# Ten small products go from VectorE to GpSimd, three weight low parts come back, and six selection steps stand earlier

## The chip, the cores and the metric

One core of one Trainium2 chip runs one program. The metric is the time of the program on the device in microseconds (us), median of several runs.

## What is computed

Two layers of a decoder trunk over 512 positions of width 1024. Each layer is `x + token_mix(rms_norm(x))`, then `x + mlp(rms_norm(x))` with a squared ReLU and 4096 hidden columns. The token mixing projects the normed input once and cuts the result into 14 parts, for three groups of heads:

```python
proj = h @ w_in
(g_q, g_k, g_v, g_gate, g_lr, d_q, d_k, d_v, i_q, i_k, i_w, m_cq, m_ckv, m_kr) = split_columns(proj)
# gated linear attention: log_a = log_sigmoid(g_lr @ up + bias) / 16; b = cumsum(log_a) in chunks of 64
q_dec = qc * exp(b);  k_inv = kc * exp(-b);  k_end = kc * exp(b_end - b)
# sparse attention: score[t,s] = sum_h iw[t,h] * relu(iq[t,h] . ik[s]); each query keeps its top 128 causal keys
_, idx = lax.top_k(score, top_k)
# latent attention: q_m = rms_norm(rms_norm(m_cq) @ w_uq), k_m likewise from m_ckv and m_kr, rotary on 32 columns of each
return jnp.concatenate([o_gla, o_dsa, o_mla], axis=-1) @ w_out
```

## The kernel before

All tensors live in SBUF with features on partitions and the 512 positions along the row. The weights of a layer come in 96 units of 128 x 1024 words in a fixed order: 24 for the input projection (`UNITS`, `N_IN`), 8 for the output projection, 64 for the MLP. SyncE loads each unit into one of two `raw` buffers. A unit is split in two: ScalarE writes its rounded high part `wh` (L952, semaphore `hi_ready`), and another engine the low part `wl = raw - wh` (`lo_ready`). TensorE then makes 3 products for each of 8 blocks of a unit (L517 to L519: low by high, high by high, high by low), 24 for a unit, into one of 8 PSUM banks. Split and use are two units apart (`AHEAD`). Low parts are made by VectorE (`low_part`, L1275) for units 0 to 7 and for those of the output projection and the MLP, and by GpSimd (L464) for the units that are used two after those in `POOL_LOW = range(6, N_IN)`, that is from 8 on.

Each engine has one queue, written out by hand and run in order. In slot `u` (0 to 23) of the input projection:

- ScalarE waits until TensorE is through with unit `u`, splits unit `u + 2`, and does its `tasks(u)`: ReLU planes for the indexer (`relevant`), squares for the norms (`square`), factors `rsqrt(mean + eps)` (`factor`, `key_factor`), the exponentials of the decays (slot 8, into `e1` and `e2`, `exp_ready`), and a scaled copy of each latent query into `tf` (`query_square`, `q_copied`).
- VectorE takes the unit out of its bank (`evacuations`), makes some selection steps (`select_steps`), and does its own `tasks(u)`: the weighted sums of the indexer's planes (`weighted`, L1401), the scan for the decays (L1478, L1480), the normed queries and keys of the sparse heads (`dsa_queries` L1362, `dsa_keys` L1367) and of the latent heads (`mla_turn`, `mla_queries`, `mla_keys`).
- TensorE runs unit `u`, and between units small fp32 products: sums of squares for the norms (`stat`, L553; the one for the key factor L608, L609), `mla_q(h)` (L587, L589), `mla_k(pr)` (L600) and `mla_v(i)` (L618). Its order is `unit(9)`, `dqst0`, `mla_q(0)`, `unit(10)`, `mqst0`, `dqst1`, `mla_q(1)`, ..., `unit(15)`, `mkst1`, `mla_v(0)`, `unit(16)`, `mla_v(1)`, `unit(17)`.

A bank is used again when its readers have freed it. `mla_v(1)` writes the bank that held `mk1`, and that is freed by the second product of `mla_keys(1)`:

```python
vec.scalar_tensor_tensor(kT[0:NOPE, 2 * pr + 1], mk[NOPE:P, :], gain(G_MKN, NOPE, P), f[NOPE:P],
                         ALU.mult, ALU.mult).then_inc(*B.on_read(f"mk{pr}"))        # L1389
```

`mla_v(0)` and `mk0` are tied in the same way. A selection step finds the 8 largest scores of each of 128 queries (MAX8, L1350) and replaces them by a mark (a MATCH_VALUE_LOAD and a MATCH_REPLACE8, L1354). 16 steps for each of the query blocks 3, 2 and 1 (rows of 512, 384 and 256 scores) make 48; in before they go round in the order 3, 2, 1, and `per_slot` spreads them over slots 9 to 22. Steps of three different blocks are issued together, since they don't wait for one another. After slot 23 come the attention heads, the output projection and the MLP, which the change doesn't touch.

Of the kernel before, what the change touches and what calls it, by code (L numbers as in the profile page):

```python
# [17 lines left out]
ALU = mybir.AluOpType  # L18
# [39 lines left out]
POOL_LOW = range(6, N_IN)  # L58
# [36 lines left out]


# [110 lines left out]
def build_trunk(nc, x_in, stream, params, consts, out):  # L207
    with ExitStack() as ctx:
# [144 lines left out]
        q_copied = S("q_copied", H)  # L353
        krb_ready = S("krb_ready")
# [76 lines left out]
        def _(pool):  # L431
# [18 lines left out]
            for l in range(DEPTH):  # L450
# [9 lines left out]
                pool.memset(gqp[:], 0.0).then_inc(zeroed.sem, 1)  # L460
                pool.wait_ge(*lo_ready.at(l, POOL_LOW[0] + AHEAD - 1))
                for u in POOL_LOW:
                    pool.wait_ge(*hi_ready.at(l, u + AHEAD))
                    pool.tensor_tensor(wl[:, u % 2], raw[:, u % 2], wh[:, u % 2], ALU.subtract)\  # L464
                        .then_inc(lo_ready.sem, 1)
                    if u == 19:
                        pool.wait_ge(*B.filled(l, "mv1"))
                        alone(pool)
                    if u in (19, 21):
                        pool.memset(ke[:, (u - 19) // 2], 0.0).then_inc(zeroed.sem, 1)  # L470
# [790 lines left out]
        def _(vec):  # L1261
# [50 lines left out]
            for l in range(DEPTH):  # L1312
# [27 lines left out]
                def select_steps(first, n):  # L1340


                    for i0 in range(first, first + n, 3):
                        queries = [3 - i % 3 for i in range(i0, min(i0 + 3, first + n))]
                        found = {}
                        for qb in queries:
                            if qb in taken:
                                vec.wait_ge(*taken[qb])
                            alone(vec)
                            found[qb] = mark(vec.max(m8[:, qb - 1], scores_of(qb)))  # L1350
                        for qb in queries:
                            vec.wait_ge(*found[qb])
                            alone(vec)
                            taken[qb] = mark(vec.match_replace(scores_of(qb), m8[:, qb - 1], scores_of(qb), TAKEN))  # L1354
# [15 lines left out]
                def mla_turn(h):  # L1370
                    vec.wait_ge(*q_copied.at(l, h))
                    vec.tensor_tensor(tf[64:QK, h % 2], tf[64:QK, h % 2], cos, ALU.mult)
                    vec.scalar_tensor_tensor(qT[64:QK, h], B[f"mq{h}"][QK:P, :], gain(G_MQ, QK, P), sin,
                                             ALU.mult, ALU.mult).then_inc(*B.on_read(f"mq{h}"))

                def mla_queries(h):

                    vec.wait_ge(*B.freed(l, f"mq{h}"))
                    link(vec.tensor_tensor(tf[64:QK, h % 2], tf[64:QK, h % 2], qT[64:QK, h], ALU.add))
                    f = use_factor(f"mqst{h}")  # L1380
                    after(vec.tensor_tensor(qT[0:QK, h], tf[0:QK, h % 2], f[0:QK], ALU.mult),
                          nrs_used.sem, nrs_used.at(l, norm_index(f"mqst{h}"))[1])
# [22 lines left out]
                def evacuations(u):  # L1405
# [42 lines left out]
                    if u in (12, 13):  # L1448
                        pr = u - 12
                        vec.wait_ge(*exp_ready.at(l, pr))  # L1450
                        vec.wait_ge(*zeroed.at(l, 0))

                        link(vec.scalar_tensor_tensor(kinv[:, pr], rb[:], GLA_DK ** -0.5, e1[:, pr],
                                                      ALU.mult, ALU.mult))
                        vec.wait_ge(*B.filled(l, f"gq{pr}"))
                        vec.tensor_tensor(gqp[0:64, 2 * pr], B[f"gq{pr}"][0:64, :], kinv[0:64, pr], ALU.mult)
                        vec.tensor_tensor(gqp[64:P, 2 * pr + 1], B[f"gq{pr}"][64:P, :], kinv[64:P, pr], ALU.mult)\
                            .then_inc(*B.on_read(f"gq{pr}"))
                    if u in (14, 15):
                        pr = u - 14  # L1460
                        link(vec.tensor_tensor(e2[:, pr], e2[:, pr], rb[:], ALU.mult))
# [6 lines left out]
                def tasks(u):  # L1468
# [5 lines left out]
                    if u == 7:  # L1474
                        weighted(3)
                        for pr in range(2):
# [6 lines left out]
                    if u == 8:  # L1483
                        f = use_factor("cqst")
# [31 lines left out]
                    if u in (14, 15):  # L1516
                        pr = u - 14
                        vec.wait_ge(*B.freed(l, f"gk{pr}"))
                        dec = e1[:, pr].rearrange("p (c t) -> p c t", t=CHUNK)[:, :, CHUNK - 1:CHUNK]
                        vec.tensor_tensor(tf[:, pr].rearrange("p (c t) -> p c t", t=CHUNK),  # L1520
                                          kinv[:, pr].rearrange("p (c t) -> p c t", t=CHUNK),
                                          dec.to_broadcast([P, NCHUNK, CHUNK]), ALU.mult)\
                            .then_inc(kend_ready.sem, 1)
                        mla_keys(pr)

                steps = 3 * (TOPK // 8)
                per_slot = {9: 3, 10: 3, 11: 3, 12: 2, 13: 2, 14: 2, 15: 2, 16: 4, 17: 4, 18: 4,
                            19: 5, 20: 5, 21: 5, 22: 4}
                done = 0
                for u in range(N_IN):  # L1530
                    if u not in POOL_LOW and (l, u) != (0, 0):
                        low_part(u % 2, hi_ready.at(l, u + AHEAD))
                    evacuations(u)
                    select_steps(done, per_slot.get(u, 0))
# [322 lines left out]
```

## Time and profile before

| | us |
|---|---|
| median of 3 runs | 1255.13 (1254.95 to 1256.62) |
| profiled execution, own time | 1253.49 |
| its span, first to last instruction | 1251.7 |
| TensorE busy | 1236.5 |
| VectorE busy | 777.6 |
| ScalarE busy | 528.5 |
| GpSimd busy | 216.7 |

Engines are named in the profile as PE (TensorE), PEld (its weight loads), DVE (VectorE), ACT (ScalarE), POOL (GpSimd) and SP (SyncE). The granted TensorE clock was 0.999 of full speed over the span. Times in rows are microseconds from the start of the span. The shown end of a matmul is modelled and lies over the start of the next; the distance of two starts is the better measure: 0.23 us within a unit.

### The profile page before, as it was taken

Reading aid. Unit: us, or ns where it says so; the run is one execution under the profiler, and the core shown is the slowest. Engines: PE = TensorE matmul, PEld = TensorE weight load, DVE = VectorE, ACT = ScalarE, POOL = GpSimd, SP = SyncE. Lnnn points to the kernel's source line nnn. Section 1 sums busy time; section 2 is a strip of 40 time slices with the busy share of each in tenths; the row PEclk is TensorE's granted clock in tenths of the full one; section 3 lists DMA queues with packets and bytes.
Section 4 is the critical chain, followed back from the end, with each engine's and each line's share of the span. In section 5 each row is a group of like instructions: output and inputs, shape, how many; then the busy total and the mean of one; then the engine's idle time right before and its main releaser. Section 6 shows DMA issues by size and latency. Waiting matters only on the chain.

```text
span 1251.7 us, 17687 instructions
## 1 busy us (share of the span) xinstructions
PE 1236.5 (99%) x5956; PEld 973.0 (78%) x5956; DVE 777.6 (62%) x1234; ACT 528.5 (42%) x858; POOL 216.7 (17%) x140
## 2 busy tenths in 40 slices
PE   8999999999999999999999999999999999999998
PEld 7766776688888888888886667767888888888887
DVE  6699988644644554544757999785446445445444
ACT  5674438643323224224437643585442242232331
POOL 1132330020120110210522234200201102102002
PEclk9999999999999999999999999999999999999999
DMA  6212220023232223322322222201232232233223
GB/s 242 89 51 68 68 85 2 17 102 116 99 101 91 95 98 101 101 84 101 101 89 81 68 68 68 69 2 46 89 101 90 96 101 101 84 101 101 95 98 109
DMA packets 30720, 108.36 MB, mean 87 GB/s; under 512 B 3536, under 2 KB 3536, under 8 KB 30672
## 3 DMA queue, kind: packets, MB, share of 16 engines
q1 hardware_dynamic: 29520, 103.82, 24.9%
q0 software_dynamic: 432, 2.86, 0.6%
q10 hardware_dynamic: 720, 1.07, 0.3%
q8 instruction: 27, 0.44, 0.2%
q14 instruction: 21, 0.17, 0.0%
HBM read 105.64 MB, written 2.10 MB: 86 GB/s over the span
## 4 chain that ended last, share of the span: by engine, by line
PE 82%; DVE 11%; issue 4%; ACT 3%; DMA 1%; ACTq 0%; DVEq 0%
PE bank L898 19%; PE bank L897 19%; PE bank L899 19%; PE bank L517 4%; PE bank L518 4%; PE bank L519 4%; PE bank L540 2%; PE bank L538 2%; PE bank L539 2%; PE bank L779 1%; PE bank L791 1%; DVE sel L1401 1%; PE bank L806 1%; DVE sel L1354 1%; DVE m L1350 1%
## 5 line engine op out<-in xcount | busy, mean ns | idle before, releaser
L952 ACT ACTIVATE wh<-raw 128x1024 fp32r<-128x1024 f32 x191 | 201.7, 1056 | 377.9 <-PE bank L899 246.5
L1275 DVE TENSOR_TENSOR wl<-raw,wh 128x1024 fp32r<-128x1024 f32 x155 | 240.5, 1552 | 75.6 <-ACT wh L952 75.5
L897 PE MATMUL bank<-hh,wl 128*128 128x512 f32 x512 | 200.0, 391 | 0.0
L897 PE MATMUL bank<-xmh,wl 128*128 128x512 f32 x512 | 199.3, 389 | 0.0
L899 PE MATMUL bank<-hl,wh 128*128 128x512 f32 x512 | 199.2, 389 | 0.0
L899 PE MATMUL bank<-xml,wh 128*128 128x512 f32 x512 | 199.2, 389 | 0.0
L898 PE MATMUL bank<-xmh,wh 128*128 128x512 f32 x512 | 199.2, 389 | 0.0
L898 PE MATMUL bank<-hh,wh 128*128 128x512 f32 x512 | 199.2, 389 | 0.0
L482 POOL TENSOR_TENSOR x<-x,rsb 128x512 f32<-128x512 f32 x62 | 82.0, 1322 | 587.4 <-DVE rsb L1696 587.4
L1685 DVE TENSOR_TENSOR sqb<-tf 128x512 f32<-128x512 f32 x64 | 44.3, 692 | 181.6 <-ACT hh L1238 181.6
L517 PE MATMUL bank<-xgh,wl 128*128 128x512 f32 x368 | 151.0, 410 | 2.7 <-DVE xgl L1288 2.5
L519 PE MATMUL bank<-xgl,wh 128*128 128x512 f32 x368 | 143.5, 390 | 0.0
L518 PE MATMUL bank<-xgh,wh 128*128 128x512 f32 x368 | 143.5, 390 | 0.0
L464 POOL TENSOR_TENSOR wl<-raw,wh 128x1024 fp32r<-128x1024 f32 x36 | 87.6, 2432 | 232.3 <-ACT wh L952 232.3
L1236 ACT ACTIVATE tf<-bank 128x512 f32<-128x512 f32 x64 | 38.3, 598 | 204.5 <-PE bank L899 204.5
L1696 DVE TENSOR_TENSOR rsb<-bank,rb 128x512 f32<-128x512 f32 x64 | 44.3, 692 | 128.0 <-PE bank L899 125.8
L897 PEld LDWEIGHTS bank<-hh,wl 128*128 128x128 f32 x512 | 96.1, 188 | 20.5 <-issue 0.5
L897 PEld LDWEIGHTS bank<-xmh,wl 128*128 128x128 f32 x512 | 96.1, 188 | 20.5 <-DVE xml L1288 0.4
L898 PEld LDWEIGHTS bank<-hh,wh 128*128 128x128 f32 x512 | 96.1, 188 | 20.2 <-issue 0.5
L899 PEld LDWEIGHTS bank<-hl,wh 128*128 128x128 f32 x512 | 96.1, 188 | 20.0
L899 PEld LDWEIGHTS bank<-xml,wh 128*128 128x128 f32 x512 | 96.1, 188 | 19.9
L898 PEld LDWEIGHTS bank<-xmh,wh 128*128 128x128 f32 x512 | 96.1, 188 | 19.8
(218 smaller groups left out, 1669.2 us busy)
## 6 DMA issues: line engine op xcount, KB each, us to landing
raw<-in_stream SPq DMA_DIRECT2D x191, 512.0 KB, 3.3
out_y<-x SPq DMA_DIRECT2D x8, 256.0 KB, 3.5
x<-in_x ACTq DMA_DIRECT2D x4, 256.0 KB, 7.0
x<-in_x SPq DMA_DIRECT2D x4, 256.0 KB, 7.1
con<-in_consts POOLq DMA_DIRECT2D x1, 976.5 KB, 5.2
par<-in_params POOLq DMA_DIRECT2D x1, 916.0 KB, 5.5
par<-in_params POOLq DMA_DIRECT2D x1, 896.0 KB, 6.9
raw<-in_stream SPq DMA_DIRECT2D x2, 256.0 KB, 4.1
```

The lines of the kernel that those rows point to most:

```text
L464: pool.tensor_tensor(wl[:, u % 2], raw[:, u % 2], wh[:, u % 2], ALU.subtract)\
L482: pool.tensor_tensor(x[:, d], x[:, d], rsb[:, d % 2], ALU.add).then_inc(x_ready.sem, 1)
L517: pe.matmul(bank[:], wk_l, act_h[:, k], start=(n == 0), stop=False)
L518: pe.matmul(bank[:], wk_h, act_h[:, k], start=False, stop=False)
L519: m = pe.matmul(bank[:], wk_h, act_l[:, k], start=False, stop=last)
L897: pe.matmul(B.t[s][:], wl[:, s, n_block(k)], src_h[:, k], start=(k == 0), stop=False)
L898: pe.matmul(B.t[s][:], wh[:, s, n_block(k)], src_h[:, k], start=False, stop=False)
L899: m = pe.matmul(B.t[s][:], wh[:, s, n_block(k)], src_l[:, k], start=False, stop=(k == KB - 1))
L952: act.activation(wh[:, s], raw[:, s], ACT.Copy).then_inc(hi_ready.sem, 1)
L1275: vec.tensor_tensor(wl[:, s], raw[:, s], wh[:, s], ALU.subtract).then_inc(lo_ready.sem, 1)
L1685: vec.tensor_tensor(sqb[:, s], tf[:, s], tf[:, s], ALU.mult).then_inc(hid_ready.sem, 1)
L1696: vec.tensor_tensor(rsb[:, s], B.t[s][:], rb[:], ALU.mult).then_inc(dn_freed[s].sem, 1)
```

## The change

`POOL_LOW` begins at 9, not 6: in slots 6, 7 and 8 VectorE makes the low parts of units 8, 9 and 10, after its evacuations. GpSimd takes ten products of each layer: the decays `e1` and `e2` times `rb` (two each, `scale_decay`), the cosine part of the four latent queries' rotation (`turn_query`, on 32 partitions), and `kend` (two, `key_end`). They stand in its queue behind its low parts of slots 9 to 15. The factor `GLA_DK ** -0.5` goes into VectorE's products that write `gqp`. Of the selection, two steps of query block 3 are made in slots 7 and 8, one in each; slots 12 to 15 have three steps in place of two, and slots 19 to 22 have 4, 4, 3, 2 in place of 5, 5, 5, 4.

```diff
-POOL_LOW = range(6, N_IN)
+POOL_LOW = range(9, N_IN)
+SELECT = [3, 3] + [3, 2, 1] * (TOPK // 8 - 2) + [2, 1] * 2
...
+        q_turned = S("q_turned", H)
+        scaled = S("scaled", 4)
...
+                def scale_decay(buf, pr):
+                    pool.wait_ge(*exp_ready.at(l, 1))
+                    src, dst = (e1, kinv) if buf == 0 else (e2, e2)
+                    pool.tensor_tensor(dst[:, pr], src[:, pr], rb[:], ALU.mult).then_inc(scaled.sem, 1)
+
+                def turn_query(h, ahead):
+                    pool.wait_ge(*ahead)
+                    pool.wait_ge(*q_copied.at(l, h))
+                    pool.tensor_tensor(tf[64:QK, h % 2], tf[64:QK, h % 2], cos, ALU.mult).then_inc(q_turned.sem, 1)
+                    pool.wait_ge(*q_turned.at(l, h))
+
+                def key_end(pr):
+                    pool.wait_ge(*B.freed(l, f"gk{pr}"))
+                    dec = e1[:, pr].rearrange("p (c t) -> p c t", t=CHUNK)[:, :, CHUNK - 1:CHUNK]
+                    pool.tensor_tensor(tf[:, pr].rearrange("p (c t) -> p c t", t=CHUNK),
+                                       kinv[:, pr].rearrange("p (c t) -> p c t", t=CHUNK),
+                                       dec.to_broadcast([P, NCHUNK, CHUNK]), ALU.mult).then_inc(kend_ready.sem, 1)
+
...
+                    if u == 9:
+                        pool.wait_ge(const_loaded, 16)
+                        scale_decay(0, 0)
+                        scale_decay(0, 1)
+                        turn_query(0, scaled.at(l, 1))
+                    if u in (10, 11):
+                        scale_decay(1, u - 10)
+                        turn_query(u - 9, scaled.at(l, u - 8))
+                    if u == 12:
+                        turn_query(3, lo_ready.at(l, u + AHEAD))
+                    if u in (14, 15):
+                        key_end(u - 14)
...
                 def mla_turn(h):
                     vec.wait_ge(*q_copied.at(l, h))
-                    vec.tensor_tensor(tf[64:QK, h % 2], tf[64:QK, h % 2], cos, ALU.mult)
...
                 def mla_queries(h):
 
                     vec.wait_ge(*B.freed(l, f"mq{h}"))
+                    vec.wait_ge(*q_turned.at(l, h))
...
                     if u in (12, 13):
                         pr = u - 12
-                        vec.wait_ge(*exp_ready.at(l, pr))
+                        vec.wait_ge(*scaled.at(l, pr))
...
-                        link(vec.scalar_tensor_tensor(kinv[:, pr], rb[:], GLA_DK ** -0.5, e1[:, pr],
-                                                      ALU.mult, ALU.mult))
...
-                        vec.tensor_tensor(gqp[0:64, 2 * pr], B[f"gq{pr}"][0:64, :], kinv[0:64, pr], ALU.mult)
...
+                        vec.scalar_tensor_tensor(gqp[0:64, 2 * pr], B[f"gq{pr}"][0:64, :], GLA_DK ** -0.5,
+                                                 kinv[0:64, pr], ALU.mult, ALU.mult)
...
-                        link(vec.tensor_tensor(e2[:, pr], e2[:, pr], rb[:], ALU.mult))
+                        vec.wait_ge(*scaled.at(l, 2 + pr))
...
                     if u == 7:
                         weighted(3)
+                        select_steps(0, 1)
...
                     if u == 8:
+                        select_steps(1, 1)
...
-                per_slot = {9: 3, 10: 3, 11: 3, 12: 2, 13: 2, 14: 2, 15: 2, 16: 4, 17: 4, 18: 4,
-                            19: 5, 20: 5, 21: 5, 22: 4}
-                done = 0
+                per_slot = {9: 3, 10: 3, 11: 3, 12: 3, 13: 3, 14: 3, 15: 3, 16: 4, 17: 4, 18: 4,
+                            19: 4, 20: 4, 21: 3, 22: 2}
+                done = 2
                 for u in range(N_IN):
-                    if u not in POOL_LOW and (l, u) != (0, 0):
+                    if u < 6 and (l, u) != (0, 0):
                         low_part(u % 2, hi_ready.at(l, u + AHEAD))
                     evacuations(u)
+                    if 6 <= u < POOL_LOW[0]:
+                        low_part(u % 2, hi_ready.at(l, u + AHEAD))
                     select_steps(done, per_slot.get(u, 0))
```

`key_end`'s product stood in VectorE's `tasks(14)` and `tasks(15)` (L1520), `turn_query`'s at L1372, `scale_decay`'s at L1453 and L1461.

## Rows read from the trace of the kernel before

**Rows 1.** The page, part 1: busy us, share of the span, instructions.

```profile
...
PE 1236.5 (99%) x5956; PEld 973.0 (78%) x5956; DVE 777.6 (62%) x1234; ACT 528.5 (42%) x858; POOL 216.7 (17%) x140
...
```

**Rows 2.** By stretch: us, busy PE, PEld, DVE, ACT, POOL (instructions), clock, DMA share, GB/s.

```profile
...
62.00:135.00 73.00, 70.81 (x268) 47.95 (x266) 70.30 (x111) 41.18 (x67) 20.90 (x9) 1.00 0.18 58
...
135.00:175.00 40.00, 40.00 (x180) 33.03 (x180) 35.78 (x99) 15.95 (x20) 17.53 (x9) 1.00 0.26 83
...
```

**Rows 3.** TensorE's waits over the whole span: total, times, longest.

```profile
...
PE bank L618 <- DVE kT L1389: 4.4, 2, 2.2
...
```

**Rows 4.** Timeline of TensorE: start, us, operation, idle before and releaser.

```profile
...
132.41 0.39 PE L519 MATMUL bank<-xgl,wh 128*128 128x512 f32 x1
134.99 1.13 PE L618 MATMUL bank<-par,ckvn 128*128 128x256 f32 x4 [2.19 <-DVE kT L1389]
...
```

**Rows 5.** The chain that ended last, 124 to 137 us.

```profile
...
126.19 2.42 DVE kT L1391
...
134.18 0.77 DVE kT L1389
...
```

**Rows 6.** Timeline of GpSimd, 40 to 150 us.

```profile
...
67.28 2.51 POOL L464 TENSOR_TENSOR wl<-raw,wh 128x1024 fp32r<-128x1024 f32 x1 [8.47 <-ACT wh L952]
74.62 2.38 POOL L464 TENSOR_TENSOR wl<-raw,wh 128x1024 fp32r<-128x1024 f32 x1 [4.83 <-ACT wh L952]
82.53 2.36 POOL L464 TENSOR_TENSOR wl<-raw,wh 128x1024 fp32r<-128x1024 f32 x1 [5.53 <-ACT wh L952]
91.46 2.36 POOL L464 TENSOR_TENSOR wl<-raw,wh 128x1024 fp32r<-128x1024 f32 x1 [6.57 <-ACT wh L952]
...
```

**Rows 7.** Timeline of VectorE, 40 to 180 us.

```profile
...
62.70 0.69 DVE L1478 SCALAR_TENSOR_TENSOR e<-tf,e 128x512 f32<-128x512 f32 x1 [1.51 <-ACT e L1088]
...
67.56 3.04 DVE L1401 SCALAR_TENSOR_TENSOR sel<-rel,iws,sel 128x256 f32<-128x256 f32 x2
...
73.75 3.53 DVE L1401 SCALAR_TENSOR_TENSOR sel<-rel,iws,sel 128x256 f32<-128x256 f32 x3
...
77.83 0.69 DVE L1330 TENSOR_TENSOR dqr<-bank,rb 128x512 f32<-128x512 f32 x1
78.44 1.47 DVE L1350 MAX8 m<-sel 128x8 f32<-128x512 f32 x3
...
81.52 0.68 DVE L1372 TENSOR_TENSOR tf<-tf,con 32x512 f32<-32x512 f32 x1
82.22 0.76 DVE L1373 SCALAR_TENSOR_TENSOR qT<-bank,par,con 32x512 f32<-32x512 f32 x1
83.01 2.43 DVE L1362 SCALAR_TENSOR_TENSOR dqn<-dqr,par,rsb 128x512 f32<-128x512 f32 x1
...
176.36 0.29 DVE L1606 CUSTOM_DVE_ANT_0 pb<-bank,con 128x128 f32<-128x128 f32 x1 [3.54 <-PE bank L779]
...
```

**Rows 8.** VectorE by line, 62 to 135 us: count, busy us, mean ns.

```profile
...
L1453 DVE SCALAR_TENSOR_TENSOR kinv<-rb,e 128x512 f32<-128x512 f32 x2 | 1.4, 680 | 0.0
...
L1485 DVE SCALAR_TENSOR_TENSOR cqn<-cqn,par,rsb 128x512 f32<-128x512 f32 x1 | 0.7, 744 | 0.0
...
```

**Rows 9.** Four lines, whole span: duration ns min/median/max, first and last start.

```profile
...
L1275 DVE TENSOR_TENSOR wl<-raw,wh x155: 1215/1226/2141, 14.0 to 1238.0; 128x1024 fp32r<-128x1024 f32 x155
...
L482 POOL TENSOR_TENSOR x<-x,rsb x62: 1287/1292/2202, 332.8 to 1243.1; 128x512 f32<-128x512 f32 x62
...
L1350 DVE MAX8 m<-sel x96: 408/545/695, 78.4 to 790.5; 128x8 f32<-128x512 f32 x32, 128x8 f32<-128x384 f32 x32, 128x8 f32<-128x256 f32 x32
...
L1354 DVE MATCH_REPLACE8 sel<-m,sel x96: 407/545/689, 79.9 to 791.2; 128x512 f32<-128x512 f32 x32, 128x384 f32<-128x384 f32 x32, 128x256 f32<-128x256 f32 x32
...
```

**Rows 10.** Timeline of TensorE at `mla_q(0)` and at `dqst1`.

```profile
...
74.03 1.02 PE L587 MATMUL bank<-cqn,par 128*128 128x512 f32 x2
...
82.06 1.02 PE L553 MATMUL bank<-sqb,con 128*128 128x512 f32 x2
...
```

**Rows 11.** Timeline of ScalarE, 40 to 140 us.

```profile
...
127.65 0.63 ACT L1043 ACTIVATE rsb<-lnb 128x512 f32<-128x512 f32 x1
...
```

More of the change, by code:

```diff
@@ L1340, in select_steps @@
                 def select_steps(first, n):
-                    for i0 in range(first, first + n, 3):
-                        queries = [3 - i % 3 for i in range(i0, min(i0 + 3, first + n))]
+                    rest = SELECT[first:first + n]
+                    while rest:
+                        queries = rest[:3] if len(set(rest[:3])) == len(rest[:3]) else rest[:1]
+                        rest = rest[len(queries):]
                         found = {}
@@ L1449, in evacuations @@
                         pr = u - 12
-                        vec.wait_ge(*exp_ready.at(l, pr))
+                        vec.wait_ge(*scaled.at(l, pr))
                         vec.wait_ge(*zeroed.at(l, 0))
-                        link(vec.scalar_tensor_tensor(kinv[:, pr], rb[:], GLA_DK ** -0.5, e1[:, pr],
-                                                      ALU.mult, ALU.mult))
                         vec.wait_ge(*B.filled(l, f"gq{pr}"))
-                        vec.tensor_tensor(gqp[0:64, 2 * pr], B[f"gq{pr}"][0:64, :], kinv[0:64, pr], ALU.mult)
-                        vec.tensor_tensor(gqp[64:P, 2 * pr + 1], B[f"gq{pr}"][64:P, :], kinv[64:P, pr], ALU.mult)\
-                            .then_inc(*B.on_read(f"gq{pr}"))
+                        vec.scalar_tensor_tensor(gqp[0:64, 2 * pr], B[f"gq{pr}"][0:64, :], GLA_DK ** -0.5,
+                                                 kinv[0:64, pr], ALU.mult, ALU.mult)
+                        vec.scalar_tensor_tensor(gqp[64:P, 2 * pr + 1], B[f"gq{pr}"][64:P, :], GLA_DK ** -0.5,
+                                                 kinv[64:P, pr], ALU.mult, ALU.mult).then_inc(*B.on_read(f"gq{pr}"))
                     if u in (14, 15):
                         pr = u - 14
-                        link(vec.tensor_tensor(e2[:, pr], e2[:, pr], rb[:], ALU.mult))
+                        vec.wait_ge(*scaled.at(l, 2 + pr))
                         vec.wait_ge(*B.filled(l, f"gk{pr}"))
@@ L1517, in tasks @@
                         pr = u - 14
[L1518 to L1523, printed above, removed]
                         mla_keys(pr)
                 steps = 3 * (TOPK // 8)
-                per_slot = {9: 3, 10: 3, 11: 3, 12: 2, 13: 2, 14: 2, 15: 2, 16: 4, 17: 4, 18: 4,
-                            19: 5, 20: 5, 21: 5, 22: 4}
-                done = 0
+                per_slot = {9: 3, 10: 3, 11: 3, 12: 3, 13: 3, 14: 3, 15: 3, 16: 4, 17: 4, 18: 4,
+                            19: 4, 20: 4, 21: 3, 22: 2}
+                done = 2
                 for u in range(N_IN):
-                    if u not in POOL_LOW and (l, u) != (0, 0):
+                    if u < 6 and (l, u) != (0, 0):
                         low_part(u % 2, hi_ready.at(l, u + AHEAD))
                     evacuations(u)
+                    if 6 <= u < POOL_LOW[0]:
+                        low_part(u % 2, hi_ready.at(l, u + AHEAD))
                     select_steps(done, per_slot.get(u, 0))
```

## The prediction

> **What bounds the kernel now.** I read the page's busy table first [rows 1]: TensorE is busy for 1236.5 of 1251.7 us, so at most 15.2 us of the span can ever come from a better order, and the question is only where its idle microseconds lie and whether this change touches them. The table of stretches [rows 2] shows a strange stretch, 62 to 135 us in the first layer, in which VectorE is busy for 70.3 of 73 us and TensorE loses 2.2 us; from 135 to 175 us TensorE loses nothing. The second layer repeats the first. The list of TensorE's waits [rows 3] says what the loss is: twice, once per layer, 2.2 us for VectorE's line 1389, which frees the bank of mk1, so that `mla_v(1)` (L618) can fill it. The timeline [rows 4] gives the size: the last product of unit 16 starts at 132.41, the next would start 0.23 later, at 132.64, and starts at 134.99, a hole of 2.35 us. The chain [rows 5] runs back from there through VectorE without a pause. Elsewhere in the stretch the chain goes through VectorE too, but TensorE's products follow one another, so VectorE's lateness has cost nothing until 132.6. That is the trap of this page: work taken off VectorE is worth 2.35 us a layer and no more, whatever its amount.
>
> **What the port does.** In the rows of both engines [rows 6, 7] a product of GpSimd on two SBUF operands and one of VectorE of the same kind never run together. GpSimd's low part at 82.53 lasts 2.36, to 84.89; VectorE's L1362, started at 83.01, takes 2.43 and ends at 85.44, where the same form at L1485 takes 0.74 [rows 8]. L1373 at 82.22, with its operand in PSUM, takes its usual 0.76, and MAX8 and MATCH_REPLACE8 are never stretched: over all 96 of each, none takes more than 0.70 [rows 9]. The Trainium skill, SBUF — State Buffer, "SBUF: two separate sides", says this as a rule: VectorE with two SBUF inputs and GpSimd exchange an exclusive lock, and the loser blocks for the whole instruction. The trace agrees with that. By the page alone, with every one of the ten products meeting such a product of VectorE, it would lose some 13 us a layer (an estimate), and the change would be a loss; by the rows it loses only where two such products meet.
>
> **The change part by part**, for the first layer (the second adds the same).
> Removed from VectorE: four L1372, two L1453, two L1461, two L1520 at 0.68 to 0.69 each (L1453 stands for them in [rows 8]), ten products, 6.8 us. Added: the two products into gqp take a scale, which I price by the neighbouring scaled form, 0.76 against 0.68 [rows 7, 8], four times 0.07 = 0.3. Added: low parts for units 8, 9 and 10 at 1.22 each [rows 9]. They take the place of three of GpSimd's 2.4 us, the last at 67.28, which stretched two L1401 to 3.04 where two take 0.98 (a neighbour takes 0.49), so 2.06 is given back there [rows 6, 7]. The low parts of 8 and 9 stand ahead of `weighted(1)` and `weighted(3)`, which on VectorE wait for ScalarE's planes, or where GpSimd held it, so I take them as even; at the worst they are 2.4 us, and then the balance below starts that much later.
> Moved: six selection steps come ahead of unit 16. A triple takes 3.08 (78.44 to 81.52 [rows 7]), a step on query block 3 alone its MAX8 and MATCH_REPLACE8, 0.70 and 0.69 at most [rows 9], and a load between them, 1.5 in all. The first lone one fills the 1.51 us in which VectorE waited for the gate at 62.70, so it costs nothing while it ends by then; without the cover it would cost 1.5. The second, at unit 8, costs 1.5. Slots 12 to 15 take four more, 4 x 1.03 = 4.1. The later slots lose six; they are no gain, as selection ended at 172.8 and VectorE then waited 3.54 us for TensorE, to 176.36 [rows 7].
>
> The balance of VectorE: before, from the end of `weighted(4)` at 71.12 (67.56 + 3.04 and one more of 0.49, with their gaps) to the end of L1389 at 134.94 it works through 63.8 us [rows 5, 7], of which the port takes 2.07 (L1401 at 73.75: 3.53 for three of 0.49), 1.69 (L1362), and so on to 1.74 (L1391 at 126.19), seven times and 11.2 in all [rows 5, 7]. So 52.6 is work. After, it starts at 67.07 + 4 x 0.51 = 69.1 and has 52.6 + 1.1 (low part 10, by its pitch) + 1.5 + 4.1 + 0.3 - 6.8 = 52.8 to do. Without a block it would be at L1389 at 121.9; TensorE asks at 132.64. So blocks and waits may add 10.7 us before the hole comes back at all.
>
> How much do they add? I follow it through. L1486 ends at 69.1 + 0.6 + 1.15 + 1.5 + 0.66 + 0.74 = 73.8; `mla_q(0)` on TensorE wants it at 74.03 [rows 10] (before: 73.16). Margin 0.2, cost 0. Then `weighted(5)`, four SBUF products from 74.4, meets the low part of 11 at 74.6 and the first two products of GpSimd behind it. Their price isn't in the trace before by name; the nearest row is GpSimd's product of the same 128x512 at L482, 1.29 [rows 9]; half of the 2.36 of the 128x1024 one is 1.18. A product on 32 partitions has the same row length; I take 1.29 for it too, and for the one with a broadcast. When both engines want the port they should alternate, since GpSimd got in at 74.7 between two L1401 that follow 0.03 us apart. So VectorE loses 2.3 + 2 x 1.3 and reaches the evacuation of dq1 at about 81.1, not 77.83 [rows 7], ends it at 81.8; ScalarE's square (0.63) follows, and TensorE's `dqst1`, which stood at 82.06, starts at about 82.45: 0.4 us lost. If VectorE wins each time it is 0; if GpSimd wins each time (low part, two scalings, first turn, 6.3 us in a row), VectorE is 1.4 later still, and it is 1.75.
> From there the selection, which needs no port, covers GpSimd's products: the first turn, `scale_decay(1, 0)` and turn 1 end by 88, under slot 10's triple. After slot 10 VectorE is at 92.3 and the low part of 91.46 blocks L1362 as it did before, to 94.4. The turns of queries 2 and 3 wait for ScalarE's copies (94.9 and 103.9) and end at some 96.8 and 105.2, before L1379 of slots 11 and 12 (98.1, 105.6); if one slips onto it, it costs 1.3. By slot 13 VectorE waits for TensorE: it is through with krot near 116 (before 120.97), takes gk0 when TensorE has it, at 116.5, and gk1 at 124.6; a triple follows, to 128.4; ScalarE's factor for mkst1, which ended at 128.28 [rows 11], is no later. So L1389 ends at about 129.9, 2.7 us before TensorE asks. `key_end` runs behind a low part (128.1 to 129.4), under products with PSUM operands.
> Waits in GpSimd's queue: behind each turn stands the next low part. It starts with ScalarE's high part, at 91.46 and 100.39, and TensorE needs it a whole unit later, 8.9 us; a turn waiting for its copy ends long before. Behind `mla_v(1)` units 17 to 23 run on TensorE without holes [rows 2], paced by nothing but TensorE, and the attention behind them waits for them; I see nothing that takes the 2.35 back.
>
> The sum, per layer: -2.35 for the hole, +0.4 at dqst1, 0 elsewhere: -1.95. Two layers: -3.9. On the profiled execution (1253.49, span 1251.70) that is 1249.6; on the median of the three runs, 1255.13, it is **1251.2**, 0.31% less.
>
> **Rivals.**
> A. *GpSimd starves VectorE at weighted(5).* The trace never shows two GpSimd products in a row against VectorE, so this stays open. Then 1.75 is lost at dqst1: -0.6 a layer, 1253.9, within 0.2%. Against it: GpSimd itself got in between two back-to-back instructions, and the reverse should hold.
> B. *VectorE stays the bound, slower.* Place: the port, between 69 and 132 us. If the 11.2 us of blocks stay and half of the eight products that come before L1389 add 1.3 each, the sum is 16.4 against the 10.7 that are free, and the hole is 5.7 instead of 2.35: +3.4 a layer, 1261.8. It decides against the change from 13.1 us of blocks on. For it: seven meetings already cost 11.2. Against it: the blocks are no sum of products but of meetings, and with VectorE ahead most meet a selection or a PSUM product.
> C. *The wait is only replaced*, so that nothing comes of it: the hole ends, but a factor of ScalarE or `mq0` (margin 0.2) is late by as much. mkst1's factor is ready at 128.28 and two products of 0.76 follow, 2.8 us ahead of need, against it; a slip of the decays behind the lone step at unit 7 speaks for it. Price: 1255.
>
> **How the numbers follow.** Forecast 0.70, A 0.12, B 0.08, C 0.10. The forecast's own range is from 2 x 2.35 with no loss at all (1250.4) to 2 x 1.3 saved (1252.5). To leave out no more than two in ten I go down to 1249.5 (the three runs before differ by 1.7) and up to 1254.3, which holds A. 0.2%, 2.5 us, is what a measurement here can tell from no change: faster, below 1252.6, holds the forecast, 0.71; same, A and C, 0.20; slower 0.09.
>
> **What the profile after would show.** TensorE's wait for L1389 gone, L618 right behind unit 16, and everything from there 2 us earlier per layer; VectorE idle before the evacuations of gq1, gk0 and gk1; selection ended near 165. A new small wait at L553 (dqst1) near 82, whose size tells alternation from starvation. GpSimd's products near 1.3. No wait of TensorE for a low part. I am wrong if L618 still waits, if `mq0` or `dqst1` waits over 1 us, or if GpSimd's products take 2 us and more.

## The result, and the profile after

The kernel after takes 1248.17 us (median of 4, 1248.05 to 1248.41), the kernel before 1255.84 in the same measurement (1254.95 to 1256.62); the ratio is 0.9938, 95% interval 0.9922 to 0.9953. That is 7.7 us less where 3.9 were forecast (1251.2, range 1249.5 to 1254.3): the right way, and too small by half.

The page of the kernel after, parts 1 and 4: busy time, and the chain by engine. Before, 11% of the chain was VectorE's and 82% TensorE's.

```profile
...
PE 1236.8 (99%) x5956; PEld 974.4 (78%) x5956; DVE 753.1 (60%) x1220; ACT 527.2 (42%) x858; POOL 227.5 (18%) x154
...
PE 93%; DVE 3%; ACT 2%; issue 1%; DMA 1%; ACTq 0%; DVEq 0%
...
```

The two stretches of [rows 2] in the kernel after, with the same columns, and TensorE's waits, the longest first:

```profile
...
62.00:135.00 73.00, 73.00 (x279) 50.36 (x278) 67.34 (x126) 42.34 (x69) 31.50 (x18) 1.00 0.17 58
135.00:175.00 40.00, 40.00 (x228) 33.01 (x229) 25.88 (x81) 16.91 (x27) 18.17 (x10) 1.00 0.27 93
...
```

```profile
...
PE bank L827 <- DVE pb L1647: 1.0, 2, 0.5
PE bank L596 <- POOL ones L437: 1.0, 1, 1.0
PE bank L553 <- DVE xgl L1324: 0.8, 2, 0.5
...
PE bank L815 <- ACT lnb L1061: 0.2, 1, 0.2
...
```

TensorE now fills the stretch, with 279 products begun in it where 268 were, and the wait of [rows 3] is gone. The timeline of TensorE after, at the two value products (L654 is what L618 was):

```profile
...
125.75 1.03 PE L654 MATMUL bank<-par,ckvn 128*128 128x256 f32 x4
...
131.87 0.39 PE L555 MATMUL bank<-xgl,wh 128*128 128x512 f32 x1
132.10 1.02 PE L654 MATMUL bank<-par,ckvn 128*128 128x256 f32 x4
132.78 0.58 PE L553 MATMUL bank<-xgh,wl 128*128 128x512 f32 x1
...
```

and the same place before, beside [rows 4]:

```profile
...
126.22 1.13 PE L618 MATMUL bank<-par,ckvn 128*128 128x256 f32 x4
127.00 0.58 PE L517 MATMUL bank<-xgh,wl 128*128 128x512 f32 x1
...
```

```profile
...
135.77 0.58 PE L517 MATMUL bank<-xgh,wl 128*128 128x512 f32 x1
```

Unit 17 begins at 132.78 in place of 135.77. Of these 2.99 us, 0.33 are the opening: TensorE is that much ahead from 11 us on, before anything that the change touches, and openings differ from execution to execution (by 0.11 between two profiles of the kernel before). 2.66 are gained in the stretch: 0.24 at `mla_v(0)`, which starts 0.14 sooner beyond the opening's part and takes 0.68 to the next unit in place of 0.78, and 2.42 at `mla_v(1)`. The second layer gains about as much at its two value products, twice 2.66 is 5.3, and the spans of the two profiled executions stand 5.4 apart (1251.7, 1246.3). The small rest is the opening's 0.33, less 0.24 that TensorE loses again in the first layer's attention, where L815 waits for ScalarE (the last line of the waits above; 219.78 us). So the two profiles account for 5.4 of the 7.7 us and know nothing of the other 2.3. They lie in the executions before: their profile is of one that took 1253.49, while the others took 1255 and 1256.6, and those after agree within 0.4. The experiments were made for that remainder first.

How VectorE comes to be in time is seen in its timeline after (the first fence) and GpSimd's (the second):

```profile
...
74.01 4.43 DVE L1439 SCALAR_TENSOR_TENSOR sel<-rel,iws,sel 128x256 f32<-128x256 f32 x3
78.48 1.41 DVE L1439 SCALAR_TENSOR_TENSOR sel<-rel_last,iws,sel 128x256 f32<-128x256 f32 x1
79.92 0.69 DVE L1366 TENSOR_TENSOR dqr<-bank,rb 128x512 f32<-128x512 f32 x1
...
91.22 2.87 DVE L1400 SCALAR_TENSOR_TENSOR dqn<-dqr,par,rsb 128x512 f32<-128x512 f32 x1
...
100.04 0.75 DVE L1405 SCALAR_TENSOR_TENSOR dkn<-dkn,par,rsb 128x512 f32<-128x512 f32 x1
...
128.74 0.76 DVE L1427 SCALAR_TENSOR_TENSOR kT<-bank,par,rsb 64x512 f32<-64x512 f32 x1
...
```

```profile
...
74.33 2.39 POOL L488 TENSOR_TENSOR wl<-raw,wh 128x1024 fp32r<-128x1024 f32 x1 [58.36 <-ACT wh L988]
76.69 2.91 POOL L470 TENSOR_TENSOR kinv<-e,rb 128x512 f32<-128x512 f32 x2
79.68 1.16 POOL L475 TENSOR_TENSOR tf<-tf,con 32x512 f32<-32x512 f32 x1
...
```

`weighted(5)` does meet GpSimd there, and the engines take turns: its four instructions take 0.47, 2.49, 1.40 and 1.41 us one by one, end at 79.89 and lose about 3.8 us: 2.0 to the low part, 0.9 to each of two products. L1400 meets the low part once more at 91.22; L1405 at 100.04, which was stretched to 2.28 before, is not touched. L1427, the old L1389, ends at 129.50, 2.6 us before TensorE asks.

### The profile page after: what moved, and what is told of

Same layout as the page of the kernel before. It is cut to its first block, busy times and chain, and to the rows that moved or that the text cites. A ratio compares the mean times of both kernels' runs of the same rounds, so it can differ in the third digit from the quotient of the medians.

```text
span 1246.3 us, 17707 instructions
## 1 busy us (share of the span) xinstructions
PE 1236.8 (99%) x5956; PEld 974.4 (78%) x5956; DVE 753.1 (60%) x1220; ACT 527.2 (42%) x858; POOL 227.5 (18%) x154
## 4 chain that ended last, share of the span: by engine, by line
PE 93%; DVE 3%; ACT 2%; issue 1%; DMA 1%; ACTq 0%; DVEq 0%
PE bank L934 19%; PE bank L935 19%; PE bank L933 19%; PE bank L553 7%; PE bank L555 7%; PE bank L554 7%; PE bank L576 2%; PE bank L574 2%; PE bank L575 2%; PE bank L589 2%; PE bank L815 1%; PE bank L827 1%; PE bank L687 1%; PE bank L842 1%; DVE pb L1640 1%
## 5 line engine op out<-in xcount | busy, mean ns | idle before, releaser
L1311 DVE TENSOR_TENSOR wl<-raw,wh 128x1024 fp32r<-128x1024 f32 x161 | 247.7, 1539 | 75.9 <-ACT wh L988 75.7
L488 POOL TENSOR_TENSOR wl<-raw,wh 128x1024 fp32r<-128x1024 f32 x30 | 72.7, 2425 | 214.6 <-ACT wh L988 214.6
```

The source lines that it names most:

```text
L1311: vec.tensor_tensor(wl[:, s], raw[:, s], wh[:, s], ALU.subtract).then_inc(lo_ready.sem, 1)
```

## The experiments

They ran in three groups of four, each group with 15 to 18 executions of the kernel before beside it on the same chip (medians 1254.92, 1255.18, 1254.98). All ratios are against these.

**1. The kernel before once more.** No edit.

> The kernel before, unchanged, profiled once more. The executions before lay between 1254.95 and 1256.62 and the profiled one at 1253.49, those after between 1248.05 and 1248.41. Theory A: VectorE's chain sets TensorE's hole ahead of L618, and where its products meet GpSimd's differs from execution to execution; then a slower execution shows a longer hole, over 2.35 us a layer, or holes at other places behind VectorE, and all kernels with VectorE on the path scatter by 1 to 3 us. Theory B: the scatter is in the opening loads or elsewhere; then the holes at L618 stay 2.35 (2.2 by the wait) in a slower execution, and variants without the hole scatter as much.

Measured: 11 executions, 1253.47 to 1257.95, median 1255.18. The 15 executions of the same kernel that ran as its counterpart fall into three groups: 5 at 1253.3 to 1253.5, 6 at 1254.9 to 1255.0, 4 at 1256.2 to 1256.8. In the third group of experiments it was the same: 4 at 1253.3 to 1253.5, 7 at 1254.7 to 1255.1, 4 at 1256.3 to 1256.8. Time doesn't scatter, it comes in steps of some 1.6 us, and TensorE's mean granted clock goes with them: over all 48 executions beside the experiments it is 0.999 to 1.000 on the lowest step, 0.998 to 0.999 on the middle one and 0.997 on the highest. The one at 1257.95 lies a step higher still, with 0.996; no profile shows where. The profiled execution took 1255.18, one step above the one of [rows 1]. Two stretches of it, with the granted clock as the third number from the end, and then the same of the profile before:

```profile
...
750.00:754.00 4.00, 1.81 (x9) 1.20 (x8) 3.95 (x10) 1.06 (x1) 1.16 (x1) 1.00 0.00 0
754.00:758.00 4.00, 4.00 (x11) 3.16 (x12) 3.97 (x6) 2.51 (x3) 1.19 (x1) 0.58 0.39 130
...
```

```profile
...
750.00:754.00 4.00, 1.82 (x8) 1.20 (x8) 3.95 (x10) 1.06 (x1) 1.25 (x1) 1.00 0.01 3
754.00:758.00 4.00, 4.00 (x19) 3.32 (x19) 3.97 (x6) 2.51 (x3) 1.10 (x1) 1.00 0.41 131
...
```

and the product behind the hole in the profile before:

```profile
...
753.76 1.13 PE L618 MATMUL bank<-par,ckvn 128*128 128x256 f32 x4 [2.18 <-DVE kT L1389]
...
```

The hole is the same (1.81 and 1.82 us busy of 4). Right behind it the granted clock is 0.58 in the one, 1.00 in the other, and TensorE begins 11 products where it began 19. In the timeline of the slower one:

```profile
...
753.86 1.36 PE L618 MATMUL bank<-par,ckvn 128*128 128x256 f32 x4 [2.19 <-DVE kT L1389]
754.66 0.99 PE L517 MATMUL bank<-xgh,wl 128*128 128x512 f32 x1
755.45 0.63 PE L518 MATMUL bank<-xgh,wh 128*128 128x512 f32 x1
755.87 0.63 PE L519 MATMUL bank<-xgl,wh 128*128 128x512 f32 x1
...
758.26 0.39 PE L519 MATMUL bank<-xgl,wh 128*128 128x512 f32 x1
758.49 0.40 PE L517 MATMUL bank<-xgh,wl 128*128 128x512 f32 x1
...
```

Starts stand 0.43 us apart from 755.45 on and 0.23 again from 758.26: the lower of the two levels, 1.2 in place of 2.4 GHz. Each product of that stretch costs 0.2 us more than at full speed, and the execution took 1.69 us more than the profiled one before (1255.18, 1253.49). Neither theory had it right. VectorE's hole isn't longer in the slower execution (2.18 and 2.19), against A; the holes stay, as B had it, but the opening makes only 0.1 of the 1.7. The hole has a second price, the clock behind it, which falls in some executions and not in others. The Trainium skill, TensorE: Matmul & The Clock Gate, "Part 1: The HAM clock gate", names the two levels and says that the array's clock is gated by TensorE's recent activity; the trace agrees, with 1.00 ahead of the hole (over 740 to 753 us) and half speed behind it.

**2. Four selection steps later.** The kernel before with

```diff
-                per_slot = {9: 3, 10: 3, 11: 3, 12: 2, 13: 2, 14: 2, 15: 2, 16: 4, 17: 4, 18: 4,
-                            19: 5, 20: 5, 21: 5, 22: 4}
+                per_slot = {9: 3, 10: 3, 11: 3, 12: 2, 13: 2, 14: 0, 15: 0, 16: 5, 17: 5, 18: 5,
+                            19: 5, 20: 5, 21: 5, 22: 5}
```

> The kernel before with the four selection steps of slots 14 and 15 moved behind slot 15 (slots 16 to 22 take five each), nothing else. Theory of the two waits (L618 waits for mk0 and mk1, freed by L1389, and nothing else of the change counts): VectorE reaches the second L1389 some 3.9 us sooner, at 131.0, before TensorE asks at 132.64, so both waits go and the time is that of the kernel after, 1248.2 within 1 us, and it scatters as little. Rival (the gain comes from the ten products and their port): the time is less than half the way, above 1252.

Measured: 1247.83 (5 executions, 1247.79 to 1249.4), ratio 0.9945, 0.9932 to 0.9959. TensorE is busy for 73.00 us of the stretch. All of the gain comes from the table of selection steps, with not one product moved to GpSimd. The one execution at 1249.4 lies 1.6 us above the other four's median, and its mean clock is 0.998 in place of 1.000: by both it looks like one fall of the clock, in a kernel that has no hole at L618. It wasn't profiled.

**3. The ten products alone.** The kernel after with

```diff
-POOL_LOW = range(9, N_IN)
+POOL_LOW = range(6, N_IN)
...
-SELECT = [3, 3] + [3, 2, 1] * (TOPK // 8 - 2) + [2, 1] * 2
+SELECT = [3, 2, 1] * (TOPK // 8)
...
-                        select_steps(0, 1)
...
-                        select_steps(1, 1)
...
```

and `per_slot` of before.

> The kernel after with the low parts of units 8 to 10 on GpSimd and the selection spread as before, so that of the change only the ten products are left. By the balance VectorE has 52.6 - 6.8 + 0.3 = 46.1 us of work from 71.1 on and 11 to 14 us of meetings at the port: it reaches L1389 at 128 to 131, in time, and the time is 1248.2 within 1 us. Rival (port): each product given away is paid back at the port, VectorE stays late, and the time stays above 1252.

Measured: 1248.28 (5, 1247.98 to 1248.34), ratio 0.9944, 0.9931 to 0.9958. As expected.

**4. All but the ten products.** The kernel before with

```diff
-POOL_LOW = range(6, N_IN)
+POOL_LOW = range(9, N_IN)
...
+SELECT = [3, 3] + [3, 2, 1] * (TOPK // 8 - 2) + [2, 1] * 2
...
+                        select_steps(0, 1)
...
+                        select_steps(1, 1)
...
-                    if u not in POOL_LOW and (l, u) != (0, 0):
+                    if u < 6 and (l, u) != (0, 0):
...
+                    if 6 <= u < POOL_LOW[0]:
+                        low_part(u % 2, hi_ready.at(l, u + AHEAD))
```

and `per_slot` of after: L1453, L1461, L1372 and L1520 stay with VectorE.

> The kernel after with the ten products back on VectorE, so that of the change the low parts and the earlier selection are left. Balance: from 69.1 on 52.8 + 6.8 - 0.3 = 59.3 us of work and some 11 us of meetings, L1389 ends at about 139.5, 7 us late in place of 2.35: 4.5 us a layer worse than before, 1264. Rival (the ten products are worth nothing because the port takes them back): as fast as the kernel after, 1248.

Measured: 1260.92 (4, 1260.63 to 1260.97), ratio 1.0045, 1.0030 to 1.0061. Worse, as the balance had it, by 6 us and not 9. TensorE waits 3.8 us for L1392 (L1389's place) ahead of `mla_v(0)` in each layer, and the clock falls behind that in both; the table of stretches, at the first layer's hole and behind the second's:

```profile
...
127.00:130.00 3.00, 0.08 (x1) 0.08 (x1) 2.95 (x5) 1.10 (x2) 0.89 (x1) 1.00 0.32 81
130.00:133.50 3.50, 3.50 (x9) 2.74 (x10) 3.43 (x6) 0.60 (x1) 0.00 (x0) 0.52 0.22 85
...
752.00:758.00 6.00, 5.98 (x14) 4.76 (x15) 5.93 (x14) 0.60 (x1) 0.00 (x0) 0.50 0.14 55
...
```

In the second layer the fall lasts longer than the one of experiment 1: the clock is at half for all of 752 to 758 us. The later hole ahead of `mla_v(1)` is gone, since the first one has let VectorE catch up. So with the low parts and the selection moved as they are in the change, the ten products are needed: they turn 1260.9 into 1248.2 (the kernel after; 1248.17, and 1248.28 in experiment 10).

**5. The hole filled.** The kernel before with 20 products that nobody reads:

```diff
                 unit(16)
+                pe.wait_ge(*B.vacant(l, "ketr1"))
+                for _ in range(20):
+                    pe.matmul(B["ketr1"][:, 0:P], ones[:], ones[:], start=True, stop=True)
                 mla_v(1)
```

> The kernel before with 20 products of 128 columns of ones, read by nobody, between unit 16 and mla_v(1): TensorE is busy for some 2.2 us in the stretch in which it waits, and VectorE's work is unchanged. The first runs showed executions of the kernel before at 1253.4, 1255.0 and 1256.7, and a profile at 1255.2 in which TensorE's granted clock fell to half for 3.4 us right behind the second hole, at a cost of 1.65. Clock theory: the hole lets the clock fall in some executions, none, one or two layers; filled, the clock stays at 1.00, all executions come together near 1253.4, with the holes' own time still paid, and the median is 1.5 to 2 us below that of before. Rival: the clock falls for another reason (what follows the hole, or chance), and the executions scatter from 1253.4 to 1256.7 as before.

Measured: 1257.37 (11, 1257.21 to 1257.70), ratio 1.0017. The time missed the expectation because I mis-sized the filling: it took 4.63 us, not 2.2, and put `mla_v(1)` at 136.94. What it was for came out: 11 executions within 0.5 us, with mean clocks of 0.999 to 1.000, while 18 of the kernel before beside them spread from 1253.16 to 1256.84.

**6. The value product behind the next unit.** The kernel before with TensorE's order changed:

```diff
                 unit(16)
-                mla_v(1)
                 unit(17)
+                mla_v(1)
```

> The kernel before with mla_v(1) behind unit 17 in place of ahead of it; VectorE and GpSimd are untouched, the order of TensorE alone differs. Theory: VectorE's lateness costs only where TensorE asks for it; asked 5.5 us later it is in time (L1389 ends at 134.9, asked at 138), so the hole goes: 1248.3 within 0.6, without scatter. Rival (VectorE is a true bound of the stretch): TensorE meets it at a later place, at gg or ketr, and most of the 7 us stays.

Measured: 1248.37 (5, 1248.26 to 1248.47), ratio 0.9945, 0.9931 to 0.9958. VectorE is as busy as before in the stretch, 70.53 of 73 us, and TensorE fills it:

```profile
...
62.00:135.00 73.00, 73.00 (x278) 50.10 (x277) 70.53 (x111) 40.95 (x67) 21.11 (x9) 1.00 0.17 58
...
```

VectorE was late for one question asked early; it did not bound the stretch.

**7. One selection step fewer ahead of it.** The kernel before with

```diff
-                per_slot = {9: 3, 10: 3, 11: 3, 12: 2, 13: 2, 14: 2, 15: 2, 16: 4, 17: 4, 18: 4,
-                            19: 5, 20: 5, 21: 5, 22: 4}
+                per_slot = {9: 3, 10: 3, 11: 3, 12: 2, 13: 2, 14: 2, 15: 1, 16: 4, 17: 4, 18: 4,
+                            19: 5, 20: 5, 21: 5, 22: 5}
```

> The kernel before with one selection step of slot 15 moved to slot 22: VectorE comes to the second L1389 some 0.7 us sooner, so the hole is 1.6 in place of 2.35; mla_v(0)'s wait of 0.1 to 0.3 stays. By TensorE's time alone: 2 x 0.7 less, 1252.0 in an execution without a fall of the clock. Clock theory: a shorter hole lets the clock fall less often; with no fall the median is 1252.0, 2.9 below before, and if falls are as frequent as before 1253.5 and scatter of 1.65.

Measured: 1251.79 (8, 1251.37 to 1252.27), ratio 0.9972, 0.9962 to 0.9983. The wait is 1.5 us in place of 2.2, and the 8 executions spread over 0.9 us, without a step, and with mean clocks of 0.999 to 1.000. The profiled one went 1.6 us below the profile before in its span (1250.1), the time of the two shorter holes; the median went 3.4 below that of before. About half of the gain of this smaller hole is the clock that stays up.

**8. The low parts alone.** The kernel before with

```diff
-POOL_LOW = range(6, N_IN)
+POOL_LOW = range(9, N_IN)
...
-                    if u not in POOL_LOW and (l, u) != (0, 0):
+                    if u < 6 and (l, u) != (0, 0):
                         low_part(u % 2, hi_ready.at(l, u + AHEAD))
                     evacuations(u)
+                    if 6 <= u < POOL_LOW[0]:
+                        low_part(u % 2, hi_ready.at(l, u + AHEAD))
```

> The kernel before with the low parts of units 8 to 10 on VectorE, nothing else of the change. Balance: VectorE starts the stretch 2.0 us sooner (no meeting at 67.3) and has 1.1 more to do, so L1389 comes 0.9 sooner if the other meetings stay, at 134.0, and the hole is 1.4: 1.9 us less in an execution without a fall of the clock, 1251.6; with falls as frequent as before 1253. Rival (with the meetings decided anew it gains all): 1248.3.

Measured: 1248.30 (5, 1247.95 to 1248.34), ratio 0.9944, 0.9930 to 0.9957: it is the expectation's rival, that all is gained. Here the balance fails. VectorE's timeline in this kernel:

```profile
...
72.77 1.51 DVE L1401 SCALAR_TENSOR_TENSOR sel<-rel,iws,sel 128x256 f32<-128x256 f32 x3
...
80.01 0.75 DVE L1362 SCALAR_TENSOR_TENSOR dqn<-dqr,par,rsb 128x512 f32<-128x512 f32 x1
81.31 0.69 DVE L1330 TENSOR_TENSOR dkn<-bank,rb 128x512 f32<-128x512 f32 x1 [0.55 <-PE bank L519]
...
87.92 0.75 DVE L1362 SCALAR_TENSOR_TENSOR dqn<-dqr,par,rsb 128x512 f32<-128x512 f32 x1
90.24 0.69 DVE L1330 TENSOR_TENSOR dkn<-bank,rb 128x512 f32<-128x512 f32 x1 [1.57 <-PE bank L519]
...
```

Before, L1401 and the first L1362 stand in [rows 7], and the second L1362 was:

```profile
...
92.08 2.28 DVE L1362 SCALAR_TENSOR_TENSOR dqn<-dqr,par,rsb 128x512 f32<-128x512 f32 x1
...
```

L1362 began at 83.01 and 92.08 before and took 2.43 and 2.28; now it begins 3 to 4 us sooner, before GpSimd's low parts of 82.44 and 91.37, and takes 0.75. The meetings of before were no sum of unlucky ones. GpSimd's low part starts on TensorE's beat, 8.9 us a slot (82.53, 91.46, 100.39); VectorE's slots with one meeting each took about the same (the stretched product began at 83.01, 92.08, 101.01), so VectorE came to the next low part at the same place, again and again. In this kernel it has no meeting at 67.3 but a low part of its own to make, and reaches L1401 1.0 us sooner than before (72.77 against 73.75). That is enough to be through with three of them before GpSimd's low part of 74.60; from there it passes in front of the low parts, all but one (L1520 at 118.82 takes 1.68), and waits for TensorE.

**9. The hole filled to measure.** As 5, with `range(9)`.

> As the kernel with the filled hole, with 9 products of ones in place of 20, since the 20 took 4.6 us and put mla_v(1) 2 us late: nine take 2.1 us and end before VectorE frees the bank. Clock theory: nothing is late any more, the clock stays at 1.00, and every execution takes what the undisturbed ones of before take, 1253.4 within 0.4: the median is 1.7 below before, by work that nobody reads. Rival: the products of ones only hid the scatter behind their own length; then executions of 1255.0 and 1256.7 are back.

Measured: 1253.44 (11, 1253.12 to 1254.97), ratio 0.9990, 0.9981 to 0.9999. Its timeline, and its stretches behind the second hole:

```profile
...
132.43 2.17 PE L715 MATMUL bank<-ones 128*128 128x128 f32 x18
134.77 1.13 PE L618 MATMUL bank<-par,ckvn 128*128 128x256 f32 x4 [0.17 <-DVE kT L1392]
...
```

```profile
...
750.00:754.00 4.00, 3.84 (x27) 3.39 (x26) 3.95 (x9) 1.06 (x1) 1.46 (x1) 1.00 0.00 0
754.00:758.00 4.00, 4.00 (x20) 3.32 (x19) 3.97 (x6) 2.51 (x3) 0.89 (x1) 1.00 0.35 135
...
```

VectorE still frees the bank as late as before, but 10 of 11 executions lie at 1253.1 to 1253.9, where only 4 of the 15 of before beside them do, and the median is 1.5 us below. One stands at 1254.97; its clock may have fallen elsewhere, but it wasn't profiled. Work that nobody reads takes 1.5 us off, with VectorE's and GpSimd's work unchanged, so the remainder of the result is the clock and not the port or the opening.

**10. The kernel after once more,** beside the others.

> The kernel after, unchanged, to stand on one chip beside the others: 1248.2, all executions within 0.5.

Measured: 1248.28 (5, 1248.23 to 1248.54), ratio 0.9947, 0.9934 to 0.9961.

**11. Low parts and later selection.** Edits 8 and 2 together.

> The kernel before with the low parts of units 8 to 10 on VectorE and the four selection steps of slots 14 and 15 later: VectorE is ahead by 2 + 4 us. Theory: TensorE has no hole left in the projection stretch, so earliness beyond the wait buys nothing: 1248.0, equal to the kernel after within 0.5. Rival (VectorE bounds the stretch in a way that TensorE's timeline hides): under 1247.

Measured: 1248.27 (5, 1248.13 to 1248.49), ratio 0.9947. Once TensorE doesn't wait, more slack on VectorE buys nothing. The lowest median is experiment 2's, 0.3 us below the kernel after's 1248.17 (0.45 below that of experiment 10). Its profile lacks the wait of 0.2 us at L815, which both profiles of the kernel after have, and experiments 3, 6, 8 and 11 lack it too. So the whole change costs TensorE some 0.2 us that none of these edits does; why ScalarE is late there, no run shows.

**12. The earlier selection alone.** The kernel before with `per_slot` of after and

```diff
+SELECT = [3, 3] + [3, 2, 1] * (TOPK // 8 - 2) + [2, 1] * 2
...
+                        select_steps(0, 1)
...
+                        select_steps(1, 1)
...
```

> The kernel before with the changed places of the selection steps alone. Balance: 1.5 us at unit 8 and 4.1 in slots 12 to 15 are added ahead of the second L1389, which comes at about 140.5, with 2 us either way for meetings at the port decided anew: the hole is 7.9 in place of 2.35, 5.6 a layer, and the clock falls in both layers in all executions (3.3 against 1.5): 1268. Rival (slack in VectorE's queue takes the six steps up): within 2 us of before.

Measured: 1261.29 (4, 1260.67 to 1262.36), ratio 1.0049, 1.0033 to 1.0064: slower, and by 6.3 us, not 13. TensorE's waits:

```profile
...
PE bank L619 <- DVE kT L1392: 7.7, 2, 3.8
...
PE bank L588 <- DVE cqn L1491: 1.0, 2, 0.5
...
```

Again the hole stands ahead of `mla_v(0)`, 3.8 us a layer, and VectorE catches up there: L1392 ends its second turn at 138.37, before TensorE asks at 138.74. Two terms were off. The seven meetings at the port are still there but cost 9.6 us in place of 11.2, the last two only 0.6 and 0.8, as VectorE comes to them late in GpSimd's low part. And TensorE's wait at `mla_v(0)` pays for both value products, which the expectation had left out. The 0.5 us at `mla_q(0)` shows how thin the margin of 0.2 was: with the lone step at unit 8, and the products at 67.4 still stretched by GpSimd's low part, it is gone.

## Why the prediction was wrong

*The step that failed* is the sentence "work taken off VectorE is worth 2.35 us a layer and no more", and with it the last one of the sum, which carried a gain read from one execution over to the median. The hole costs its own length, and in about three executions of four (35 of the 48 that ran beside the experiments lie on a higher step, with a lower mean clock) TensorE's clock also falls, once or twice, at 1.6 us each. One such fall is in a profile, behind the second layer's hole (experiment 1); that the others lie behind the holes too is read from what ends them: a smaller hole, a filled one, none. The profile before was one without a fall. Its own time was 1.64 us below the median that I started from, I had both numbers, and took the difference for an offset that the change would keep. It is one fall, and it went (experiments 7, 9, 10). In the numbers of the result: 5.4 us lie between the two profiled executions, nearly all of it the holes, and the median before, 1255.84, stands 2.35 above the profiled 1253.49, between one and two falls; together 7.7. Of the 3.8 us by which the forecast gain was too small, the falls are 2.35 and three smaller terms of the sum, which follow, 1.4.

*The hole:* right in place, cause and size (2.35; 2.42 with the product's own start). *mla_v(0)*: I saw it start late and left it out of the sum; it is 0.24 a layer. *dqst1:* I charged 0.4 for the meeting at `weighted(5)`. The alternation is as predicted, but a turn of GpSimd costs VectorE 0.9 and not 1.3 (`turn_query` and `key_end` take 1.06 to 1.16; `scale_decay` takes 1.47 and 1.75, with its own waiting for VectorE in it), the evacuation came at 79.92 and not 81.1, and `dqst1` starts at 81.73, 0.33 sooner than before by the opening alone: 0. With these three terms mended the sum is -5.3 and not -3.9. *Behind the holes* I saw nothing that takes time back; L815 takes 0.24 once.

*The walk through VectorE* held within half a microsecond from the low part of 91 us on: L1427 ends at 129.50 (129.9 forecast), the low part at 91.19 blocks L1400 to 94.1 (94.4), and VectorE then waits for TensorE. *The balance* did not: in rival B, and in the expectations of experiments 4 and 8, it kept 11.2 us of meetings as a fixed charge. The kernel after had 6.1 us of them (3.8 at `weighted(5)`, 0.1 and 2.1 at L1400), well inside the 10.7 that were free and far from rival B's 16.4; experiment 8 had 1.0. Rival A did not happen: VectorE gets its turn. Rival C did not either; `mla_q(0)` kept its margin, 0.2 us, and lost it only where GpSimd's low part at 67.3 stays (experiment 12).

*What of the change earns the time:* the low parts alone (8) or the ten products alone (3) bring all of it, and so do fewer selection steps ahead of the hole (2), which is the opposite of what the change does with them. The earlier selection costs 6 us if it stands alone (12). The change spends part of what it gains on VectorE for selection steps that had no need to be early.

*Open:* what decides in one execution whether the clock falls. The hole is the same to 0.01 us with and without a fall; with holes of 2.35 the times and mean clocks speak for none, one or two falls in an execution, with holes of 1.5 for none in 8 executions, and holes of 3.8 had a fall in both layers in the two profiles taken of them. The execution at 1249.4 in experiment 2 speaks for a fall without this hole.

## What to carry to other kernels

When the profiled execution is faster than the median by more than the noise, find out what the others do before carrying a sum over: list the executions in order with their mean clocks, and see whether they stand in steps. A wait of TensorE costs its length and, in some executions, a stretch at half clock behind it; a change that makes a small hole smaller can bring twice what the trace shows (experiment 7: 3.4 us by the medians, 1.6 by the profiles). And an engine that is busy for 96% of a stretch is a bound only if someone waits for it at the end: asking later (experiment 6), or moving work that is not yet due behind what is, was worth as much as taking ten products off it.

## What the runs showed of the hardware

- Behind a hole of 2.2 to 3.8 us TensorE's granted clock fell from 1.00 to half, for 3.4 us or so (0.58 over 754 to 758 us behind 2.2) and, in the second layer of experiments 4 and 12, for 6 us or so behind 3.8 (0.50 over 752 to 758 us in experiment 4). Behind 2.2 it fell in some executions and not in others of the same kernel with the same hole. With nine fp32 products of ones in the hole, 18 passes in 2.17 us, 10 of 11 executions took the time of those without a fall.
- Two engines in a fixed beat can lock their meetings at the SBUF port: seven stretched instructions in 64 us, by 1.3 to 2.1 us each, all but one gone when VectorE came to the first of them 1.0 us sooner. When both wanted the port at once, they took turns instruction by instruction (74 to 80 us in the kernel after). The Trainium skill, SBUF — State Buffer, "Who interferes with whom", says that issue order decides who blocks, and experiment 8 shows how much hangs on it: 0.75 against 2.43 us for the same L1362.
- 20 fp32 products of 128 columns took 4.63 us on TensorE, as 40 passes, 0.23 for each product (experiment 5).
